# Attention probabilities turned unscaled: reciprocals spread by small products and applied to the output of a pair of heads

## The reference: what is computed

```
  h = RMSNorm(x);  [x_rec | x_gate | c_q | c_kv | k_rot | g_rec | g_att] = h @ W_in
  rec = gelu(x_gate) * RG-LRU(causal_conv4(x_rec))
  att = MLA(c_q, c_kv, k_rot)   # chunk-causal, QK-norm, 16 heads x 64
  x  += W_out( sigmoid(g_rec) * rec + sigmoid(g_att) * att )
```

```
    s = jnp.einsum('bqhd,bkhd->bhqk', q, k).astype(jnp.float32) * (QK_DIM ** -0.5)
    s = jnp.where(visible[None, None], s, -jnp.inf)
    p = jax.nn.softmax(s, axis=-1).astype(v.dtype)
    return jnp.einsum('bhqk,bkhd->bqhd', p, v)
```

## Time and profile before

| | us |
|---|---|
| median of three runs | 3554.67 |
| the profiled execution | 3555.15 |
| its span | 3553.4 |
| PE busy in the span | 3033.6 (85%) |
| DVE busy | 1633.9 (46%) |
| ACT busy | 982.0 (28%) |
| POOL busy | 327.2 (9%) |

### The profile page before, as it was taken

One profiled execution on the slowest core, in us unless ns is written; L12 is line 12 of the kernel. 1 busy time (PEld: TensorE's weight loads), 2 busy tenths in 40 slices (PEclk: granted clock), 3 DMA queues, 4 the chain that ended last, 5 costly groups with the idle time before them and its releaser, 6 DMA issues.

```text
span 3553.4 us, 46204 instructions
## 1 busy us (share of the span) xinstructions
PE 3033.6 (85%) x17332; PEld 2522.5 (71%) x17332; DVE 1633.9 (46%) x3308; ACT 982.0 (28%) x1680; POOL 327.2 (9%) x459
## 2 busy tenths in 40 slices
PE   3888688888789999998889687888888699999996
PEld 2888577678788999997888576768888444444442
DVE  4666566665554433346675566665553200000001
ACT  1333244443333222122433244443332000000000
POOL 3000122220000000000000222220000100000001
PEclk9999788778888999998999777878888699999998
DMA  4212100002222222222122000002221589989985
GB/s 152 84 59 75 30 8 16 8 0 85 72 82 71 72 72 84 73 73 75 59 61 69 23 16 8 8 0 97 95 77 31 219 296 318 318 313 317 317 313 180
DMA packets 219142, 384.43 MB, mean 108 GB/s; under 512 B 34534, under 2 KB 156454, under 8 KB 218992
## 3 DMA queue, kind: packets, MB, share of 16 engines
q1 hardware_dynamic: 202640, 329.80, 28.1%
q0 software_dynamic: 16352, 52.67, 4.2%
HBM read 352.99 MB, written 29.44 MB: 108 GB/s over the span
## 4 chain that ended last, share of the span: by engine, by line
PE 69%; DVE 15%; issue 7%; ACT 6%; POOL 1%; DMA 1%; DVEq 0%; ACTq 0%; POOLq 0%
PE ACC L361 15%; PE ACC L363 14%; PE ACC L362 14%; PE ACC L765 12%; PE TP L765 6%; DVE TR L1384 2%; PE TP L515 1%; PE TP L361 1%; PE TP L786 1%; DVE nwt L1209 1%; PE TP L523 1%; PE ACC L530 1%; PE TP L362 1%; PE TP L363 1%; PE TP L535 1%
## 5 line engine op out<-in xcount | busy, mean ns | idle before, releaser
L361 PE MATMUL ACC<-XH,WH 128*128 128x288 f32 x1984 | 594.8, 300 | 46.1 <-DVE XP L1252 37.0
L363 PE MATMUL ACC<-XH,WL 128*128 128x288 f32 x1984 | 595.2, 300 | 0.0
L362 PE MATMUL ACC<-XL,WH 128*128 128x288 f32 x1984 | 595.2, 300 | 0.0
L765 PE MATMUL ACC<-MW,XT 128*128 128x512 f32 x1024 | 445.2, 595 | 1.1 <-ACT XT L1129 1.1
L361 PEld LDWEIGHTS ACC<-XH,WH 128*128 128x128 f32 x1984 | 380.1, 192 | 49.9 <-DVE XP L1252 38.5
L821 ACT ACTIVATE WH<-RAW 128x2048 fp32r<-128x2048 f32 (+1 forms) x129 | 238.1, 1845 | 539.3 <-PE ACC L363 534.8
L362 PEld LDWEIGHTS ACC<-XL,WH 128*128 128x128 f32 x1984 | 379.6, 191 | 0.0
L363 PEld LDWEIGHTS ACC<-XH,WL 128*128 128x128 f32 x1984 | 378.4, 191 | 0.0
L765 PEld LDWEIGHTS ACC<-MW,XT 128*128 128x128 f32 x1024 | 194.6, 191 | 240.6 <-issue 239.0
L1173 DVE TENSOR_TENSOR WL<-RAW,WH 128x2048 fp32r<-128x2048 f32 (+1 forms) x129 | 284.3, 2204 | 107.7 <-ACT WH L821 106.6
L1792 DVE SCALAR_TENSOR_TENSOR HT<-HT,ACC 128x1024 f32<-128x1024 f32 x16 | 19.5, 1222 | 657.3 <-ACT HT L1135 657.3
(11 more groups left out here) (454 smaller groups left out, 5864.0 us busy)
## 6 DMA issues: line engine op xcount, KB each, us to landing
MW<-in_moe_w_dram SPq DMA_DIRECT2D x192, 1024.0 KB, 5.4
RAW<-in_w_in_dram SPq DMA_DIRECT2D x36, 1024.0 KB
RAW<-in_ffn_w_dram SPq DMA_DIRECT2D x30, 1024.0 KB
dispatched<-ZT POOLq DMA_DIRECT2D x4, 2048.0 KB, 17.7
RAW<-in_w_out_dram SPq DMA_DIRECT2D x8, 1024.0 KB
RAW<-in_w_mk_dram SPq DMA_DIRECT2D x8, 1024.0 KB
RAW<-in_w_mv_dram SPq DMA_DIRECT2D x8, 1024.0 KB
RAW<-in_w_mq_dram SPq DMA_DIRECT2D x8, 1024.0 KB
```

Of the source, the lines that this page charges most:

```text
L361: nc.tensor.matmul(out, a[0], b[0], start=first, stop=False)
L362: nc.tensor.matmul(out, a[0], b[1], start=False, stop=False)
L363: return nc.tensor.matmul(out, a[1], b[0], start=False, stop=last)
L765: mm = nc.tensor.matmul(out[:, h, :], lhs[:, 2 * pair + j, :], MW[n % RING][:, j, h * 512:(h + 1) * 512], start=(pair, j) == (0, 0), stop= ...
```

## The change

The probabilities are transposed as the exponentials leave them: PE waits only until ACT has done with the score bank, and the exponentials themselves now free that bank. The scaling on DVE is gone. Once a head, late in `attend`, DVE adds the new tokens' two partial sums and takes all reciprocals of the head (`row_sums`). Once a pair, PE spreads these over 64 output partitions for each head by ten small fp32 products with the identity (`row_scales`, two TP banks). `head_output` multiplies by the gate while it reads PSUM, `rows_scaled` multiplies by the spread reciprocals and by 0.5, and adds REC, which the recurrent branch now forms with a factor of 0.25; so the factors on ACT and in `mixed_low` go. `mixed_low` stands later.

```diff
@@ PE
+                def row_scales():
+                    t.skip("r_inv", 1)
+                    pe.wait_ge(s["r_inv"], t.next("r_inv").n)
+                    banks = open_tp(), open_tp()
+                    for bank, tiles in zip(banks, ((0, 1, 2, 3), (4,))):
+                        for k, tt in enumerate(tiles):
+                            n = rows(tt)
+                            for h in range(2):
+                                mm = nc.tensor.matmul(bank[h * 64:h * 64 + 64, k * P:k * P + n],
+                                                      sm[0:n, 32 + 8 * h + tt:33 + 8 * h + tt].to_broadcast([n, 64]),
+                                                      ident[0:n, 0:n], start=True, stop=True)
+                        mm.then_inc(s["tp_ready"], 1)
...
                     bank = open_acc()
+                    exp01 = t.last("acc", 2)
...
                         weighted_values(1 - head)
+                        if head == 0:
+                            row_scales()
                     if head == 0:
                         turn_keys(1)
...
-                    pe.wait_ge(s["p01"], t.next("p01").n)
+                    pe.wait_ge(s["acc_free"], exp01)
...
-                    pe.wait_ge(s["p23"], t.next("p23").n)
+                    pe.wait_ge(s["acc_free"], exp23)
...
                 weighted_values(1)
+                row_scales()
@@ ACT
-                    ins_.then_inc(s["p_exp"], 1)
+                    ins_.then_inc(s["acc_free"], 1)
...
-                    fn(YH[:, bass.ds(tile, 1), :], AO[:].rearrange("p (a b) -> p a b", a=1), ACT.Copy, scale=0.25)\
+                    fn(YH[:, bass.ds(tile, 1), :], AO[:].rearrange("p (a b) -> p a b", a=1), ACT.Copy)\
@@ DVE, recurrent branch
-                    v.tensor_tensor(G[:, :, 0:SEQ], G[:, :, 0:SEQ], TI[:, :, 0:SEQ], ALU.mult)
+                    v.scalar_tensor_tensor(out=G[:, :, 0:SEQ], in0=G[:, :, 0:SEQ], scalar=0.25, in1=TI[:, :, 0:SEQ], op0=ALU.mult, op1=ALU.mult)
...
@@ DVE, attention
-                def head_output(head):
+                def head_output(head, tile):
...
-                    v.tensor_copy(AO[mine, 0:SEQ], bank[mine, :]).then_inc(s["tp_free"], 1)
+                    v.scalar_tensor_tensor(out=AO[mine, 0:SEQ], in0=gate[:, 0:SEQ], scalar=1.0, in1=bank[mine, :], op0=ALU.add, op1=ALU.mult)\
+                        .then_inc(s["tp_free"], 1)
...
-                def gated_sum(tile, m):
+                def rows_scaled(m, tile):
                     dve.wait_ge(s["tp_free"], m.at(4))
+                    for cols in (slice(0, SEQ), slice(SEQ, T)):
+                        bank, m = take_tp()
+                        ins_ = v.scalar_tensor_tensor(out=AO[:, cols], in0=AO[:, cols], scalar=0.5, in1=bank[:, 0:cols.stop - cols.start],
+                                                      op0=ALU.mult, op1=ALU.mult).then_inc(s["tp_free"], 1)
+                    dve.wait_ge(s["tp_free"], m.at(4))
...
+                    v.tensor_tensor(ao, ao, REC[:, bass.ds(tile, 1), :], ALU.add).then_inc(s["mix_sum"], 1)
...
+                def row_sums(head):
+                    step(v.tensor_tensor(sm[0:NEW, 20:21], sm[0:NEW, 20:21], sm[0:NEW, 21:22], ALU.add))
+                    v.reciprocal(sm[:, 32 + 8 * head:32 + 8 * head + TT], sm[:, 16:16 + TT]).then_inc(s["r_inv"], 1)
@@ DVE, attend
-                    dve.wait_ge(s["p_exp"], t.next("p_exp").n)
-                    v.reciprocal(sm[:, 32:34], sm[:, 16:18])
...
-                    for k in range(2):
-                        v.tensor_scalar(P01[k], P01[k], sm[:, 32 + k:33 + k], None, ALU.mult)
-                    v.tensor_scalar(P0[:], P0[:], sm[0:NEW, 36:37], None, ALU.mult).then_inc(s["p01"], 1)
                     if not first:
-                        m = head_output(1 - head)
+                        m = head_output(1 - head, tile)
+                        if head == 0:
+                            rows_scaled(m, tile)
...
-                    v.tensor_scalar(P23[0][:], P23[0][:], sm[:, 34:35], None, ALU.mult)
-                    v.tensor_scalar(P23[1][:], P23[1][:], sm[:, 35:36], None, ALU.mult).then_inc(s["p23"], 1)
...
-                    if tile is not None:
-                        gated_sum(tile, m)
...
-                    if tile is not None:
-                        mixed_low(tile)
...
                     turned(lambda b: [(PTL[:, 3:13:3, :], b.rearrange("p (a b) -> p a b", a=4), PTH[:, 3:13:3, :])])
+                    if not first and head == 0:
+                        mixed_low(tile)
+                    dve.wait_ge(s["acc_free"], m23.at(2))
+                    row_sums(head)
                     if following:
                         query_scales()
```

More of the change, by code:

```diff
@@ L117 @@
     ('mix', 'pe'): dict(unit=4, acc=8, xc_lo=1, tp=8),
-    ('att', 'pe'): dict(q_lo=4, acc=18, v_lo=2, tp=40, p01=4, q_sq=4, p23=4, ka=2, unit=2),
+    ('att', 'pe'): dict(q_lo=4, acc=18, v_lo=2, tp=44, q_sq=4, r_inv=4, ka=2, unit=2),
     ('out', 'pe'): dict(unit=2, acc=4),
@@ L122 @@
     ('mix', 'act'): dict(acc=8, unit=4, xc=1, g_z=1, tp=8, g_gelu=1, lru_w=1),
[L123 removed]
+    ('att', 'act'): dict(acc=18, s_max=8, tp=44, unit=2, mix_sum=2, v_lo=2),
     ('out', 'act'): dict(acc=4, unit=2),
@@ L569, in attend @@
                     bank = open_acc()
+                    exp23 = t.last("acc", 2)
                     prompt_scores(bank, 0, 2)
@@ L994, in attend @@
                     if not first:
-                        t.skip("tp", 2)
+                        t.skip("tp", 4 if head == 0 else 2)
                     if head == 0:
@@ L1034, in _ @@
                 split_high()
-                t.skip("tp", 2)
+                t.skip("tp", 4)
                 t.skip("v_lo", 1)
@@ L1498, in negative_max @@
                                                   op0=ALU.mult, op1=ALU.mult)
[L1500 removed]
+                def head_output(head, tile):
                     mine = slice(head * 64, head * 64 + 64)
+                    gate = TGA[mine, bass.ds(tile, 1), :].rearrange("p o t -> p (o t)")
                     bank, m = take_tp()
[L1503 removed]
+                    v.scalar_tensor_tensor(out=AO[mine, 0:SEQ], in0=gate[:, 0:SEQ], scalar=1.0, in1=bank[mine, :], op0=ALU.add, op1=ALU.mult)\
+                        .then_inc(s["tp_free"], 1)
                     bank, m = take_tp()
[L1505 removed]
+                    v.scalar_tensor_tensor(out=AO[mine, SEQ:T], in0=gate[:, SEQ:T], scalar=1.0, in1=bank[mine, 0:NEW], op0=ALU.add, op1=ALU.mult)\
+                        .then_inc(s["tp_free"], 1)
                     return m
[L1508 removed]
+                def rows_scaled(m, tile):
                     dve.wait_ge(s["tp_free"], m.at(4))
[L1511 removed]
+                    for cols in (slice(0, SEQ), slice(SEQ, T)):
[3 more added lines that the diff above has]
+                    dve.wait_ge(s["tp_free"], m.at(4))
                     ao = AO[:].rearrange("p (a b) -> p a b", a=1)
[L1513 to L1515 removed]
+                    v.tensor_tensor(ao, ao, REC[:, bass.ds(tile, 1), :], ALU.add).then_inc(s["mix_sum"], 1)
                 def mixed_low(tile):
@@ L1588, in _ @@
                     for pair in range(2):
-                        attend(1)
+                        attend(1, tile=i * 2 + pair)
                         attend(0, tile=i * 2 + pair)
-                attend(1, split=0)
+                attend(1, tile=6, split=0)
                 attend(0, tile=6, last=True)
-                attend(1, last=True)
+                attend(1, tile=7, last=True)
                 split_low()
-                gated_sum(7, head_output(1))
+                rows_scaled(head_output(1, 7), 7)
                 mixed_low(7)
```

15 lines of the change are left out of this document (5 added, 10 removed).

## The result

The changed kernel took 3569.96 us (median of 6 runs, 3567.16 to 3579.40) against 3554.59 us for the kernel before (6 runs): a ratio of 1.0048, interval 1.0035 to 1.0062. It is slower by 15.4 us; the forecast had 26 us. The profiled execution took 3570.54 us, 15.4 above that of the kernel before.

A forecast was written before the change was run, and what follows sets the result against it. PE was taken to bound the even half, with waits on DVE in the odd half. The terms summed to 13.2 us a layer, +26.4 for two, on the profiled 3555.15 us: forecast 3581 us, range 3552 to 3604.

The forecast's parts named there:

- even halves: First head of each attention pair, attend(0), cut at score products: PE-bound, 2.2 us longer, six ordinary ones a layer, 13.2.
- first heads: First head of each layer: only the queries' earlier start, without waiting for the scaling, counts: -0.4 us a layer.
- odd halves: Second head of each attention pair, attend(1), where PE has waits: -0.2 us a pair, seven a layer, -1.4.
- last even halves: Last even half of a layer: 2.1 us back from the gated sum against 2.2 paid, +0.1 a layer.
- layer ends: From the last weighted value to the output projection: about 3.7 us becomes 5.4, +1.7 a layer.
- The spread products: row_scales on PE, between weighted values and turned keys: 20 instructions at 0.11 us, 2.2 us a pair.
- Rival B: In row_scales the two heads' products run side by side, about half the term: 3564 us, chance 0.20.
- Rival A: Freed DVE shortens the even half's KTL wait, scores keep the high clock: 2.7 us a pair, 3543 us, chance 0.18.
- A's sign: Rival A is decided where the even half's wait for KTL falls below 1.53 us, the wait ahead of line 535.
- Rival C: Freed DVE time gains nothing in the odd half; QTL, PTL, POOL's keys set pace: 17 us more, 3598, chance 0.16.

The follow-up runs named there:

- e4: The changed kernel with the loop of spread products (row_scales) issued twice, the second pass writing the same values: 3594.6 us.
- e3: The changed kernel with row_sums moved to right behind queries_low and mixed_low back in its old place: 3576.3 us.
- e12: The changed kernel with 18 unread products in PE's wait ahead of the even half's scores, none ahead of the queries: 3535.3 us.
- e10: e8 with 12 instead of 18 unread products ahead of the queries, and 6 more ahead of the odd half's last turned group: 3520.27 us.
- e8: e3 with 18 unread products ahead of the odd half's queries and 18 ahead of the next scores: 3503.13 us.
- e1: The changed kernel with only mixed_low back in its old place, ahead of the third turned group: 3584.8 us, median of five runs.
- e2: The changed kernel with only row_sums moved, to right behind queries_low and ahead of the PTL lows: 3569.6 us.

## Why the prediction was right, and where its terms were off

The sign, the place and the bound (PE in the even half) were right; four terms had other sizes. Three of the errors (even halves -6.3, first heads -3.1, odd halves -2.7) go the same way and make up the 11 us by which the forecast was too high. Both layers, forecast against the profiled executions:

| term | forecast, us | measured, us |
|---|---|---|
| 12 ordinary even halves | +26.4 | +20.1 |
| last even halves | +0.2 | -0.1 (22.41 to 21.28 and 22.11 to 23.16: near by chance) |
| 14 odd halves | -2.8 | -5.5 |
| layer ends (last head's first score product to the output projection) | +3.4 | +3.3 (24.18 to 26.83 and 24.05 to 24.68) |
| first heads | -0.8 | -3.9 |
| elsewhere | 0 | +1.5 |
| sum | +26.4 | +15.4 |

*The spread products: mis-sized.* "The stationary side is only 64 columns wide here, so I take 0.11" failed: 0.064, 1.28 us for 20. (The second pass of e4 has 1.00, 0.050 each, so 0.28 us of the first is not the steady pace; no run separates what it is. The low clock that the working gives for line 408 is read from the pace: the products behind it follow at 0.24 us and, from 79.15 on, at 0.13; the granted clock on record there is 1.00.) Rival B's mechanism has a part in it: with the heads apart the pace is 0.089, so alternating halves save 0.49 of 1.77 us. The Trainium skill says that tiles of the array can load and multiply in parallel ("TensorEngine Tiling (Array Packing)", Key Properties); these runs agree in direction, but the two heads' products did not take half of the time that they take apart. That all of it is paid, PE being the bound, e4 shows.

*The even halves: right for the wrong reason in part.* A half without a second slow stretch is 24.55 us before and 25.91 after, +1.36 or 16.3 in twelve; the other 3.8 of the 20.1 come from halves with such a stretch, or with longer slow scores, which take 26.2 to 29.6 us. The forecast had no term for that, and its too high pace covered it: that its 26.4 is near the 20.1 is in part luck.

*The odd halves: a small gain as forecast, the wrong limit.* Queries 0.69 later and SQ 0.61 earlier came as forecast, and -0.40 a half is near the -0.2. What the step did not see is that the query products now bound the half. They take 4.04 us behind a wait of 2.94, at a granted clock of 0.58, and SQ waits 2.87 us for their squares; before, SQ had no such wait, for the scaling held it up. With the waits filled in both kernels the change is worth -1.79 per odd half. The exponentials' first bank ends 1.13 us later in the half, as forecast (1.1), but by other parts: `mixed_low`, the add and the reciprocal take 1.57 us (618.25 to 619.82), since the add is long here, and `query_scales` gives 0.42 back, since its own long step is gone. Taking the delay away in e3 did not pay, because the even half's clock took the gain.

*The first heads and the ends.* The first heads gained 1.9 each where 0.4 was forecast; the queries' wait accounts for about 0.5, the rest is a slow stretch of the kernel before (22.9 us at a clock of 0.82, 20.98 at 0.88 after). The ends came out in sum, not each: +2.65 and +0.63 where +1.7 was forecast for both. The spread products there take 2.38 us in the first layer, at a granted clock of 0.50, and 1.35 in the second at 1.00; the first end, beside the earlier trace rows:

```profile
849.58 0.60 PE L361 MATMUL ACC<-YH,WH 128*128 128x288 f32 x1 [3.16 <-DVE YL L1545]
```

*Rival A* named the mechanism that matters most in this kernel, but put it in the wrong hands: the freed DVE does not shorten the wait for KTL (3.09 and 3.45 us, 2.92 before), so the scores stay at 1.2 GHz; filling that wait wins 2.75 us per even half (e12), close to A's 2.7. A's sign, a wait below 1.53 us, would not have told: behind 0.52 us ahead of the same transposes the granted clock is 0.50 as well (634.60 to 636.00). *Rival C* did not happen. What stays open is what sets the second slow stretch of an even half, in which PE is busy, and so what clock an even half will get.

## What to carry to other kernels

Cost a change in a pair of stages where one is bound by PE and the other leaves it idle with the clock as a term of its own: here a microsecond won in the idle stage came back as slower scores in the next, and only the lengths of the halves, not the total, showed it. To tell work from clock, fill PE's waits with unread products in both versions and compare those. Work taken from DVE pays only once what stands next in the chain, here PE's queries at 1.2 GHz, is fast enough to use it.

## What had not been expected of the hardware

- 36 products per pair that nobody reads, in waits that exist anyway, made the kernel before 1.15% and the changed one 1.7% faster (0.888 to 0.912, and 0.891 to 0.916 of the clock); a third filling made it worse (3520.3 us in e10, 3503.1 in e8).
- A DVE operation on 64x1 or 128x5 elements, 0.14 to 0.2 us elsewhere, takes 0.56 to 0.78 in one place of the odd half, whichever operation stands there (L1550 in the changed kernel, L1226 in e1 and e2, L1209 in the kernel before). In these four profiles it always lies beside POOL's sum over KA and ends with it: at 616.52 beside 616.50 in the kernel before, at 619.68 beside 619.67 in the changed one. No run moves POOL's sum, so the cause is not shown, though the expectation of e1 names POOL:

```profile
618.33 1.34 POOL L1914 TENSOR_TENSOR KA<-KA 128x288 f32<-128x288 f32 x1
```
- The 20 instructions of fp32 products with 64 stationary columns follow at 0.064 us when they alternate between output partitions 0 to 63 and 64 to 127, and at 0.089 when they don't.
